# Gated linear attention in a decoder step: the low parts of the weights, on GpSimd or on VectorE

## What is computed

```
h = rmsnorm(x) @ w_in_odd                # 1088 x 1024 times 1024 x 3088
q, k, v, gd, r = split(h)                # 4 heads: q, k 128 wide, v 256 wide
logg = log_sigmoid(gd @ gate_up + gate_b) / 16
for each chunk of 64 tokens (8 for the samples):
    b = cumsum(logg)
    o = causal(q, k, decay(b)) @ v + (q * exp(b)) @ S
    S = exp(b_last) * S + (k * exp(b_last - b)).T @ v
out = rmsnorm(o) * silu(r);  out @ w_out_odd
```

## Time and profile before

| | before |
|---|---|
| median of 3 executions | 3405.35 us (3396.54 to 3405.91) |
| profiled execution | 3402.22 us, its span 3400.2 us |
| TensorE busy | 3210.9 us (94% of the span) |
| VectorE (DVE) busy | 2117.7 us (62%) |
| ScalarE (ACT) busy | 1195.8 us (35%) |
| GpSimd (POOL) busy | 218.3 us (6%) |
| mean granted TensorE clock | 0.979 |
| GLA mixer | about 2115 to 2577 us of the span |

### The profile page before, as it was taken

One profiled execution on the slowest core, in us unless ns is written; L12 is line 12 of the kernel. 1 busy time (PEld: TensorE's weight loads), 2 busy tenths in 40 slices (PEclk: granted clock), 3 DMA queues, 4 the chain that ended last, 5 costly groups with the idle time before them and its releaser, 6 DMA issues. The chain is left out here.

```text
span 3400.2 us, 68248 instructions
## 1 busy us (share of the span) xinstructions
PE 3210.9 (94%) x28575; PEld 2750.4 (81%) x28575; DVE 2117.7 (62%) x3500; ACT 1195.8 (35%) x2251; POOL 218.3 (6%) x183
## 2 busy tenths in 40 slices
PE   8899898899888988999999999999999999999999
PEld 5666666755456658899999999888888999999999
DVE  4565756632267765777777778634425777777877
ACT  3233231211156654433334334423323433333332
POOL 0000000020400011000000000311211000000000
PEclk9999999999999989999999999999999999999999
DMA  3000000030320024133224534111214122223544
GB/s 112 17 21 15 24 12 15 13 140 24 90 77 1 2 76 156 60 125 118 97 97 140 185 133 151 52 52 40 76 47 177 56 96 97 96 97 119 183 141 148
DMA packets 122221, 286.79 MB, mean 84 GB/s; under 512 B 30700, under 2 KB 42796, under 8 KB 119228
## 3 DMA queue, kind: packets, MB, share of 16 engines
q1 hardware_dynamic: 110636, 260.94, 21.9%
q0 software_dynamic: 6928, 20.45, 2.0%
q10 hardware_dynamic: 4352, 1.05, 0.1%
HBM read 209.02 MB, written 77.50 MB: 84 GB/s over the span
## 5 line engine op out<-in xcount | busy, mean ns | idle before, releaser
L450 PE MATMUL ps<-ff_sets,ff_sum_high 128*128 128x272 f32 x4224 | 722.1, 290 | 22.9 <-DVE resid L796 10.2
L450 PEld LDWEIGHTS ps<-ff_sets,ff_sum_high 128*128 128x128 f32 x4224 | 605.1, 189 | 26.1 <-issue 25.8
L450 PE MATMUL ps<-ff_sets,ff_quarter_high 128*128 128x272 f32 x3168 | 539.4, 289 | 0.3
L450 PEld LDWEIGHTS ps<-ff_sets,ff_quarter_high 128*128 128x128 f32 x3168 | 451.3, 188 | 2.3 <-issue 1.6
L450 PE MATMUL ps<-ff_sets,ff_sum_low 128*128 128x272 f32 x2112 | 438.7, 289 | 0.0
L450 PEld LDWEIGHTS ps<-ff_sets,ff_sum_low 128*128 128x128 f32 x2112 | 334.5, 190 | 0.0
L796 DVE TENSOR_TENSOR resid<-resid,ps 128x544 f32<-128x544 f32 x368 | 258.5, 719 | 118.5 <-PE ps L450 103.0
L450 PE MATMUL ps<-ff_sets,ff_quarter_low 128*128 128x272 f32 x1584 | 327.2, 288 | 0.0
L714 DVE TENSOR_TENSOR ff_sum_low<-ff_sums,ff_sum_high 128x512 fp32r<-128x512 f32 (+1 forms) x264 | 175.6, 672 | 196.1 <-ACT ff_sum_high L568 196.1
L568 ACT ACTIVATE ff_sum_high<-ff_sums 128x512 fp32r<-128x512 f32 (+1 forms) x264 | 160.6, 615 | 378.2 <-PE ps L450 295.5
L450 PEld LDWEIGHTS ps<-ff_sets,ff_quarter_low 128*128 128x128 f32 x1584 | 249.2, 188 | 0.0
(11 more groups left out here) (648 smaller groups left out, 5887.3 us busy)
## 6 DMA issues: line engine op xcount, KB each, us to landing
ff_sets_raw<-hidden_sets SPq DMA_DIRECT2D x70, 544.0 KB, 4.6
hidden_sets<-resid SPq DMA_DIRECT2D x22, 1088.0 KB, 5.1
ff_raw<-in_wg SPq DMA_DIRECT2D x44, 512.0 KB, 6.2
ff_raw<-in_wu SPq DMA_DIRECT2D x44, 512.0 KB, 4.3
ff_raw<-in_wd SPq DMA_DIRECT2D x32, 512.0 KB, 5.1
hidden_sets<-resid SPq DMA_DIRECT2D x22, 544.0 KB, 2.9
rw_w<-in_w_rwkv SPq DMA_DIRECT2D x14, 512.0 KB, 3.5
parked_tokens<-resid SPq DMA_DIRECT2D x12, 544.0 KB, 3.3
```

What stands on the lines that cost most here:

```text
L450: mm = pe.matmul(ps[:, bank + c, 0:CHUNK], u[:, j, :], set_of(z, v, q)[:, CHUNK * c:CHUNK * c + CHUNK], start=(first and j == 0 and x == 0 ...
```

## The change

GpSimd no longer subtracts; it keeps only the wait for `low_done` and the load of unit u + 2. VectorE runs the same subtraction, with the same waits, at fixed places of its own program: units 0 and 1 inside the first third of the opening (before the drafts 2 and 7), unit 2 after that third, and the others at the step where `next_units` has them, ahead of the step's other VectorE work; the two of V8 are moved to F0 and F1.

```diff
         @block.gpsimd
         def _(pool):
-            def low(u):
-                pool.wait_ge(s.high_done, u + 1)
-                if u >= GLA_SLOTS:
-                    used(pool, u - GLA_SLOTS)
-                pool.tensor_tensor(b.low[:, u % GLA_SLOTS, :, :], b.stage[u % 2][:, :, :], b.high[:, u % GLA_SLOTS, :, :].bitcast(F32), ALU.subtract)\
-                    .then_inc(s.low_done, 1)
+            def load_behind(u):
                 if u + 2 < len(units):
                     pool.wait_ge(s.low_done, u + 1)
                     pool.dma_start(*weights(u + 2)).then_inc(here[u % 2], 16)
...
             for u in range(GLA_SLOTS):
-                low(u)
+                load_behind(u)
...
                     for u in next_units(h, x):
-                        low(u)
+                        load_behind(u)
...
+            def low(u):
+                dve.wait_ge(s.high_done, u + 1)
+                if u >= GLA_SLOTS:
+                    used(dve, u - GLA_SLOTS)
+                dve.tensor_tensor(b.low[:, u % GLA_SLOTS, :, :], b.stage[u % 2][:, :, :], b.high[:, u % GLA_SLOTS, :, :].bitcast(F32), ALU.subtract)\
+                   .then_inc(s.low_done, 1)
+
+            def lows(h, x):
+                if x in ("F0", "F1"):
+                    return next_units(h, "V8")[int(x[1]):int(x[1]) + 1]
+                return next_units(h, x) if x != "V8" else []
...
                 for k in range(KT + 1):
+                    if c == 0 and k == 2:
+                        low(0)
+                    if c == 0 and k == KT - 1:
+                        low(1)
                     if k < KT:
...
+                if c == 0:
+                    low(2)
             dve.wait_ge(g.const_here, 32)
...
+                    for u in lows(h, x):
+                        low(u)
                     if x == ("N4" if h in (1, 2) else "K2"):
                         logs(n)
                         shifts()
```

## The result

**3421.66 us**, the median of 6 executions (3417.78 to 3422.43), against 3399.86 for the kernel before beside it (3396.53 to 3405.91): a ratio of 1.0062, 95% interval 1.0051 to 1.0072. The change costs 21.8 us, 0.6%. Direction and range were right; the forecast of +12.4 us was too small. The forecast time of 3416 us looks nearer than that, because it was counted from a median of three, 3405.35, which lay 5.5 us above the 3399.86 of the six here. The profiled execution took 3422.4 us, its span 3420.7 at a mean granted clock of 0.975 (3400.2 and 0.979 before).

What follows compares the result with a forecast made beforehand. TensorE was taken to bound the kernel, GpSimd's subtractions being hidden, with VectorE's program order the cost. Terms 1.2 + 2.0 + 5.2 + 2.3 + 1.7 gave +12.4 us: 3414.6 or 3417.7, taken as 3416, range 3404 to 3425.

Steps and rivals of the forecast that it cites:

- Opening: Opening: GpSimd's holds on VectorE go, so TensorE ends G2 1.9 us sooner, later spent in the wait ahead of V4.
- V4 +1.2: Phase -1 up to V4: unit 4's subtraction ahead of `logs` waits for ScalarE's rounding and delays V4; +1.2 us.
- F steps +2.0: Phase -1: F0 and F1 wait for units 6 and 7, TensorE stops before F5, S0 starts later; +2.0 us.
- S5 5.2: Phases 0 to 2: S4's states wait behind Q2's unit, stalling S5 by 1.7 us three times; +5.2 us.
- S1 2.3: Phases 1 and 2: S0's states move behind the subtraction after R5, S1 1.15 us later twice; +2.3 us.
- what costs nothing: Unit 8 at K2 of phase 0, N2 to N4, units at V8 and R2's, loads: delays covered by TensorE's other work.
- The clock +1.7: One half-clock stretch on TensorE behind the longer wait ahead of V4; +1.7 us, bounds 0 to 8.5.
- Rival 2: More of the clock: stalls at F5 and S5 bring it down too; +14 to +19 us, 3418 to 3424; chance 0.17.
- Rival 1: The covers hold: subtractions fit VectorE's idle time, stalls half or less; 0 to 6 us, 3405 to 3411; chance 0.33.
- Rival 3: GpSimd's hold on VectorE was the bound, so the change is faster: -3.3 us, 3402; chance 0.06.
- Rival 4: It does not do what it says, e.g. subtraction stays at 2.5 us on VectorE: +9 us on top, 3425; chance 0.02.
- The clock gate's rule: TensorE: idleness lowers the clock to 1.2 GHz for a while, so every long stall would carry its own price.

Runs made afterwards that it cites:

- e8: Kernel before, GpSimd still subtracting, but VectorE waits for the same two signals at the change's places from phase -1 on: 3412.89 us, ratio 1.004.
- e0: The changed kernel once more, no edit: 3422.05 us, ratio 1.0068 against the kernel before.
- e4: Changed kernel, but units 6 and 7 subtracted behind S1 of phase 0 instead of ahead of F0 and F1: 3415.68 us, ratio 1.0046.
- e1: Changed kernel, but in phases 0 to 2 Q2's unit subtracted behind S4's state updates instead of ahead: 3414.51 us, ratio 1.0047.
- e2: Changed kernel, but R5's unit subtracted behind S1's state updates of the next phase instead of ahead of S0's: 3414.94 us, ratio 1.0044.
- e6: Kernel before, but units 0 to 2 alone subtracted by VectorE, in the opening as in the change: 3401.47 us, ratio 1.0003.
- e3: Changed kernel, but unit 4 of phase -1 subtracted inside `logs`, before the scan, instead of ahead of `logs`: 3416.18 us, ratio 1.0046.
- e7: Changed kernel with unread spare products on TensorE where it waits ahead of V4, F4 and F5 in phase -1: 3418.0 us, ratio 1.0064.
- e10: The kernel before once more, no edit, for its profile: 3400.06 us (one execution).
- e5: Changed kernel with the four moves of e1 to e4 together: 3401.19 us, ratio 1.0005 against the kernel before.
- e11: The same kernel as e5 once more, for its profile: 3405.45 us (one execution).
- e9: e5 plus unit 3 subtracted after L2 (phase -1) and K2's units of phases 1 and 2 behind S3's states: 3399.12 us, ratio 0.9997.

## Why the prediction was right, and where it was wrong

**What bounds the kernel: right.** TensorE does; 61.9 us of subtractions taken off GpSimd bought nothing, and VectorE's idle share was no shelter, since what counts is its order. e8 shows it: waits with no work behind them cost 0.4%.

**Opening, "1.9 us won, so far": 1.4 measured** (L1 comes 30.36 us after G0, 31.75 before), and only 0.4 to 0.6 in the eight kernels whose opening has a half-clock stretch, as the one before has. The wait ahead of V4 "grows to some 3.7 us", and 3.80 were measured. That the gain is "spent in this wait" was not so: the wait is 3.80 to 3.81 us whether the opening won 1.4 us (after, e0, e4) or 0.4 to 0.6 (e1, e2), V4 starts later by what the opening won less (58.53 against 59.34 and 59.50), and in e6 the gain came through whole. The wait grows by 3.2 us because of unit 4's place alone (0.82 in e3), and the opening's gain is to be taken off.

**V4 +1.2: 1.84,** which is 3.2 less 1.4; behind the slower opening of e1 and e2 it is 2.7 and 2.8. The mechanism was right, and its size hangs on the opening's 1.9: G2 ends some 0.5 us later than forecast, unit 4's rounding ends at 2165.69 and not at "about 2165.2", and the exponentials start at 2176.95 against 2175.14 before. The 9.9 us for `logs` and `shifts` without holds measured 9.9.

**F steps +2.0: 2.37. S5 5.2: 5.50. S1 2.3: 2.60.** The three mechanisms were right in engine and signal, and each sum was good to 0.4 us in this profile. In detail: TensorE waits ahead of F4 as well as F5 (0.91 and 0.87 us), and the rest of the 2.37 is clock, so that F0 to S0 takes 7.6 to 8.3 us in the five profiles with these two waits (after, e0 to e3). S5's waits are 1.75, 1.37 and 1.36 us and not three times 1.7 (which is 5.1, not 5.2); the 0.34 missing in phases 1 and 2 is waited ahead of S4, where the prediction had K2's units among what costs nothing. In sum the terms of waiting were 10.7 us and measured 12.3. e1 to e4 remove each of the four stalls alone.

**The clock +1.7: the term that failed.** "I take one such stretch" was the error: it is 8.6 us by the half-clock time, five stretches' worth (one more at V4, two at S0, one at S5 of phase 0, one at each S1, and one fewer in the opening), and sits just above the upper bound of 8.5. The argument took only the longest new wait as being like the 2.36 us of the opening, and let the shorter ones go free. What the runs show in its place: with waits of 6.2 to 13.7 us in the mixer its half-clock time is 23.9 to 30.7 us (eight profiles: after, e0 to e4, e7, e8), with waits of 2.6 us or less it is 10.2 to 17.1 (before, e10, e5, e11, e6, e9), and there is no overlap. All forecast terms, with the clock as measured, give 10.7 + 8.6 = 19.3 us, against 20.4 in the mixer.

**Rivals.** Rival 2 (more of the clock, +14 to +19) named the right term and was still small; its places were half right, as S5 of phase 0 has a stretch, S5 of phases 1 and 2 have none, and stretches came at S0 (1.3 us behind F5's wait, but in e4 too, where F5 doesn't wait) and at S1, which it didn't name. Rival 1 (covers hold) fell: the stalls came at nearly their full size. Rival 3 (the hold was the bound) fell in the changed kernel, in e6, where the holds of the opening are gone, no wait is added and the time is 1.0003, and most clearly in e5 and e9, where no hold and hardly a wait is left and the time is 1.0005 and 0.9997. The holds were real, and two of them were on TensorE's path (the wait of 2.36 us in the opening is 1.34 in e6; the scan's hold in phase -1 stood in the chain to V4's 0.59 us), but they are worth about 1 us there. Rival 4 is excluded by 1224 ns.

**The clock gate's rule**, which the prediction took from the Trainium skill (TensorE: Matmul & The Clock Gate), was given one sentence and no weight in the sum: "every long stall of the sum would carry a price of its own" would have given five times 1.7 us, 8.5, which is what was measured. The places differ, so the agreement in size is partly luck.

**Still open.** Where a half-clock stretch falls, and how long it is, changes between profiles of one kernel with equal waits (S0 to S2: 14.51 and 16.09 us before; S5 to S6: 9.18 and 7.64 after), and e6 has 17.1 us of it with the waits of before. That many waits go with much half-clock time is shown; which wait causes which stretch is shown for V4 alone. S0 to S2 in particular took 16.9 to 17.8 us in e0 to e4, e6 and e8, and 14.5 only in before and e5, and no edit separated its causes: not tried were spare products in front of S1 and S5, since all banks are in use there.

## What to carry to other kernels

When work moves to an engine that takes its instructions in order, price the waits that it brings with it before its length: here the subtraction got twice as fast, and waiting for its input in front of states that were ready cost 0.4% even with the work left out. Put such an instruction behind the last output that a busier engine needs; the same 25 subtractions, eight of them put further back, cost nothing that the time shows. And where TensorE is the bound, add to the sum of its new waits a term for the clock, here 8.6 us on 12.3 us of stalls, and do not expect to get it back by removing one wait of several.

## What was not expected of the hardware

- **Clock loss outside the mixer.** The time at half clock in the rest of the kernel, which is the same code in all of these, is between 117 and 143 us from one profile to the next (133 before, 141 after, 125 in e5), and the rest itself (span less mixer) takes 2944.2 to 2950.6 us. The two rise together, by some 0.2 us for each us at half clock. Times of single edits are to be read with this in mind: the profiled executions of e1 to e4 have a rest 3.1 to 5.7 us shorter than the changed kernel's 2949.9, beside mixers shorter by 0.9 to 5.5 us. Their medians lie 5.5 to 7 us below the changed kernel's; that this is the same sum is argued, not shown.
- **The hold by GpSimd is nearly the same for other kinds of VectorE instructions.** In e6, as in the kernel before, GpSimd's subtraction falls on VectorE's scan, whose free price is in the changed kernel. e6, then after (timelines):

```profile
2162.80 4.47 DVE L3442 TENSOR_TENSOR_SCAN gl_cum<-const,gl_shifted 128x1088 f32<-128x1088 f32 x1
```

```profile
2170.03 2.43 DVE L3436 TENSOR_TENSOR_SCAN gl_cum<-const,gl_shifted 128x1088 f32<-128x1088 f32 x1
```

Some 2.0 to 2.2 us again, for the three kinds met here: 0.73 becomes 2.95, 0.55 becomes 2.56, 2.43 becomes 4.47. By the Trainium skill (SBUF — State Buffer, on the exclusive lock of the shared port pair) one engine holds the pair for its whole instruction; these rows agree, since no hold is longer than the GpSimd subtraction beside it (2.4 to 3.0 us).
